# Output projection of a hybrid layer: who makes the low parts of w_out, in which order tile 1's halves run, and when one expert's weights are asked for

## The reference

```python
xn = rmsnorm(x, norm_mix_g) * (1 + sc1) + sh1
y_conv, y_ret = short convolution group, retention group of xn @ w_in      # 512 + 512 columns
out = jnp.concatenate([y_conv, y_ret], axis=-1) @ w_out                   # 1024 x 1024, fp32
x = x + g1 * out
xn = rmsnorm(x, norm_ffn_g) * (1 + sc2) + sh2
x = x + g2 * hier_moe(xn)       # top-1 of 4 groups, then top-2 of its 8 experts; SwiGLU, D_EXPERT 256
```

## Time and profile before

| | |
|---|---|
| time, median of 3 runs | 668.73 us (667.97 to 671.67) |
| the profiled execution's own time | 670.74 us |
| its span in the profile | 669.1 us |
| PE busy | 612.7 us (92%) |
| DVE busy | 318.4 us (48%) |
| ACT busy | 154.1 us (23%) |
| POOL busy | 160.4 us (24%) |
| granted PE clock, mean | 0.968 of full |
| DMA | 183.83 MB, 275 GB/s over the span |

### The profile page before, as it was taken

How to read it: one execution, slowest core, us unless ns; L and a number is a source line. 1 busy time by engine, 2 the same in 40 slices (tenths; PEclk the granted TensorE clock), 3 DMA queues, 4 the chain that set the end, 5 groups by cost and what they waited for, 6 DMA issues and landing times.

```text
span 669.1 us, 9054 instructions
## 1 busy us (share of the span) xinstructions
PE 612.7 (92%) x3712; PEld 437.3 (65%) x3712; DVE 318.4 (48%) x631; ACT 154.1 (23%) x297; POOL 160.4 (24%) x124
## 2 busy tenths in 40 slices
PE   3799999999999989999699899999998788889796
PEld 3579999988888865744588797555554444445342
DVE  1433118706240445718768763455454555334326
ACT  5325432122312233354221111101101000001014
POOL 0042724333242200027330011222221111111110
PEclk9989999999999999999799889999999888899999
DMA  7985240320303269788552798999999999999977
GB/s 278 387 295 219 70 153 1 126 89 37 126 0 126 69 227 394 255 317 323 190 196 89 292 390 331 414 418 418 420 417 417 418 420 417 421 417 418 416 279 299
DMA packets 50381, 183.83 MB, mean 275 GB/s; under 512 B 5861, under 2 KB 6037, under 8 KB 38945
## 3 DMA queue, kind: packets, MB, share of 16 engines
q1 hardware_dynamic: 42156, 161.59, 61.9%
q0 software_dynamic: 7216, 18.99, 7.9%
q10 hardware_dynamic: 964, 2.63, 1.1%
HBM read 172.79 MB, written 16.81 MB: 283 GB/s over the span
## 4 chain that ended last, share of the span: by engine, by line
PE 66%; DMA 20%; DVE 7%; SPq 4%; ACT 2%; issue 1%; DVEq 0%; POOLq 0%; ACTq 0%
PE bank L1138 12%; PE bank L1139 11%; PE bank L1140 11%; PE bank L1488 9%; DMA ring<-in_w_up_e 8%; DMA arena_ab<-in_w_up_e 4%; DMA x<-in_w_up_e 4%; PE bank L1508 4%; PE bank L1097 3%; DMA ring<-expert_out_rows 2%; PE bank L1433 2%; PE bank L1114 2%; DVE out_lo L480 1%; SPq L519 1%; PE bank L1192 1%
## 5 line engine op out<-in xcount | busy, mean ns | idle before, releaser
L1488 PE MATMUL bank<-ring,arena_ab 128*64 128x256 f32 x352 | 83.3, 392 | 10.1 <-DMA ring<-in_w_up_e 9.6
L680 POOL TENSOR_TENSOR w_lo<-ring,w_hi 128x1024 fp32r<-128x1024 f32 x25 | 61.4, 2458 | 112.5 <-ACT w_hi L864 112.5
L1492 PE MATMUL bank<-ring,arena_ab 128*64 128x256 f32 x352 | 83.3, 392 | 0.0
L1488 PEld LDWEIGHTS bank<-ring,arena_ab 128*64 128x64 f32 x352 | 48.9, 141 | 46.8 <-DMA ring<-in_w_up_e 17.5
L1622 DVE TENSOR_TENSOR arena_ab<-arena_ab,bank 64x256 f32<-64x256 f32 x32 | 19.5, 610 | 113.3 <-ACT arena_ab L1045 113.3
L1138 PE MATMUL bank<-arena_ab_r,w_hi 128*128 128x320 f32 x192 | 62.2, 324 | 3.0 <-DVE xn_lo L1622 2.9
L786 POOL DMA_INDIRECT expert_out_rows<-arena_ab,row_out x32 | 32.0, 1001 | 130.9 <-DVE arena_ab L1622 130.9
L1138 PE MATMUL bank<-w_hi,arena_ab_r 128*128 128x512 f32 x160 | 63.3, 396 | 0.0
L1139 PE MATMUL bank<-w_lo,arena_ab_r 128*128 128x512 f32 x160 | 62.9, 393 | 0.0
L1140 PE MATMUL bank<-w_hi,xn_lo 128*128 128x512 f32 x160 | 62.8, 393 | 0.0
L1139 PE MATMUL bank<-xn_lo,w_hi 128*128 128x320 f32 x192 | 59.9, 312 | 0.0
(11 more groups left out here) (289 smaller groups left out, 1123.1 us busy)
## 6 DMA issues: line engine op xcount, KB each, us to landing
ring<-in_w_ada SPq DMA_DIRECT2D x11, 2048.0 KB, 12.3
ring<-in_w_down_e SPq DMA_DIRECT2D x22, 1024.0 KB, 25.8
ring<-in_w_gate_e SPq DMA_DIRECT2D x22, 1024.0 KB, 23.1
ring<-in_w_up_e SPq DMA_DIRECT2D x22, 1024.0 KB, 26.0
ring<-in_w_in SPq DMA_DIRECT2D x6, 2048.0 KB, 8.4
arena_ab<-in_w_down_e SPq DMA_DIRECT2D x15, 512.0 KB, 24.0
x<-in_w_gate_e SPq DMA_DIRECT2D x5, 1024.0 KB, 25.8
arena_ab<-in_w_gate_e SPq DMA_DIRECT2D x5, 1024.0 KB, 24.0
```

The source lines that it names most:

```text
L680: pool.tensor_tensor(as_piece(w_lo[p_ % 2], p_), piece_of(w, p_), as_piece(w_hi[p_ % 2], p_), ALU.subtract).then_inc(w_lo_ready, 1)
L1488: pe.matmul(bank[2 + p_][0:BLK, 0:DE], lhs, w_gate(s)[:, kt, :], start=(kt == 0), stop=(kt == KT - 1))
L1492: last = pe.matmul(bank[2 + p_][BLK:2 * BLK, 0:DE], lhs, w_up(s)[:, kt, :], start=(kt == 0), stop=(kt == KT - 1))
```

## The change

All eight low pieces of w_out are made by DVE: four of half 0 after `residual(0, 0)`, four of half 1 after the first product of tile 1. POOL keeps only the low parts of y, and those of tile 1 are written over tile 0's place, once tile 0's products are over. In tile 1 half 1 comes first, as whole fp32 like tile 0, and half 0 follows as split. In tile 2 both halves run before `router_T(1)`. After the last tile `clock(14)` becomes `clock(5)` and `clock_on(5)` becomes `clock_on(2)`. SP asks for expert 2's gate and up (slot 0) before expert 1's (slot 2) and before tile 4's residual rows are stored.

```diff
-        out_low_done = lambda half: (1, 5)[half]
-        y_low_done = lambda t: (3, 7, 9, 11)[t - 1]
+        y_low_done = lambda t: 2 * t
+        split_half = lambda t, half: t >= 2 or (t == 1 and half == 0)
+        turn_of = lambda t, half: 2 * t + (1 - half if t == 1 else half)
@@ y_part: the low part of tile 1 lies in tile 0's place
+            to = 0 if t == 1 else t
             if group == 0:
-                return yconvT[:, :, P * t:P * t + P], yconv_lo[:, :, P * t:P * t + P]
-            return yretT[:, t, :, :], yret_lo[:, t, :, :]
+                return yconvT[:, :, P * t:P * t + P], yconv_lo[:, :, P * to:P * to + P]
+            return yretT[:, t, :, :], yret_lo[:, to, :, :]
@@ SP
             down_part_of(3, 0)
+            released(sp, e_slot[2], FIRST_EXPERT_ITEM)
+            gate_up_of(2)
             released(sp, e_slot[1], FIRST_EXPERT_ITEM)
             gate_up_of(1)
             residual_rows_out(NT - 1)
-            released(sp, e_slot[2], FIRST_EXPERT_ITEM)
-            gate_up_of(2)
@@ POOL, y_low and what follows it
                     pool.wait_ge(high_act, y_high_done(t, group))
+                    if t == 1:
+                        pool.wait_ge(wout_mm, 2)
...
-            pool.wait_ge(high_act, out_high_done(0, 3))
-            pool.wait_ge(wout_mm, 1)
-            out_low_part(pool, 0, 3).then_inc(low_pool, 1)
             y_low(1)
-            pool.wait_ge(high_act, out_high_done(1, 3))
-            pool.wait_ge(wout_mm, 2)
-            for c in (2, 3):
-                out_low_part(pool, 1, c).then_inc(low_pool, 1)
             y_low(2)
@@ PE, project
-                n = 2 * t + half
+                n = turn_of(t, half)
...
-                if t == 1:
+                if n in (3, 5):
                     pe.wait_ge(high_act, out_high_done(half, 3))
-                    pe.wait_ge(low_dve, (3, 5)[half])
-                    pe.wait_ge(low_pool, out_low_done(half))
+                    pe.wait_ge(low_dve, 4 * half + 4)
...
-                    if t >= 1:
+                    if split_half(t, half):
@@ PE, the tiles
-                project(t, 0)
+                project(t, int(t == 1))
...
-                if t == 1:
-                    project(t, 1)
+                if t in (1, 2):
+                    project(t, t - 1)
...
-                elif t != 1:
+                elif t not in (1, 2):
                     project(t, 1)
@@ PE, after the last tile
-            clock(14)
+            clock(5)
             router_T(NT - 1)
...
-            clock_on(5)
+            clock_on(2)
@@ DVE
-                residual(t, 0)
+                residual(t, int(t == 1))
+                if t == 1:
+                    dve.wait_ge(high_act, out_high_done(1, 3))
+                    for c in range(4):
+                        out_low_part(dve, 1, c).then_inc(low_dve, 1)
...
-                    for c in range(3):
+                    for c in range(4):
                         dve.wait_ge(high_act, out_high_done(0, c))
                         out_low_part(dve, 0, c).then_inc(low_dve, 1)
...
-                residual(t, 1)
+                residual(t, int(t != 1))
-                if t == 0:
-                    dve.wait_ge(high_act, out_high_done(1, 1))
-                    for c in range(2):
-                        out_low_part(dve, 1, c).then_inc(low_dve, 1)
```

## The result

The changed kernel takes 667.6 us (median of 20 runs, 663.8 to 671.17), the kernel before, beside it, 669.46 us (20 runs, 667.97 to 672.36). The ratio is 0.9971, with an interval of 0.9958 to 0.9983: about 1.9 us faster, where I had forecast 659.4 (657.1 to 663.2). That is less than the 0.5% which the prediction took as the least that can be told from no change; with 20 runs a side the interval leaves out 1, so a small gain is there. The profiled execution of the changed kernel took 665.88 us with a span of 664.1, 1.7 us less than its median, and that of before took 1.3 us more than its own. The two traces differ by 4.9 us where the medians differ by 1.9, so the traces are read for places and the medians for sizes. One number stands out at once: the runs of the changed kernel spread over 7.4 us, those of before over 4.4.

The account below looks back on a forecast made before the run. The weight stream was taken to bound the end, so expert 6's request, set by PE's work from output projection to expert 0, moves it: -6.8 - 1.3 - 1.2 = -9.3 us from 668.73 gives 659.4 us, range 657.1 to 663.2.

Parts of the forecast that it names:

- The projection: Tiles 0 to 2: reordered halves and DVE's low parts bring `router_T(0)` 7.23 us sooner, less 0.4 in tile 2: -6.8 us.
- SP's order: After the projection: asking for expert 2's gate and up sooner only fills a pause before 381.09, worth 0.
- The first gather: Slower rival at POOL's first gather, chance 0.05: 2.1 MB more ahead in the DMA engines make `gathered_rows` wait, 675.7 us.
- The request for expert 6 sets the end: At expert 0's gate and up: from 410.37 weights pass at a full queue, so the end moves with that request.
- and the same at the end: From expert 0's gate and up to the end: the summed gain of -9.3 us arrives unchanged.
- clock(14) to clock(5) and clock_on(5) to clock_on(2): After the last tile, fewer fillers let the transposes and `ranks(4)` begin sooner: -1.3 and -1.2 us.
- the low-clock stretch: From 382 to 390 us: 3.4 us at 1.2 GHz stay in place, and the transposes falling in cost 0.7 us more.
- the ratio 1.78: Price of the lower clock, from a filler's 0.20 us against 0.1125, applied to the transposes after the last tile.
- the fillers were holding the clock up: Rival after the last tile, chance 0.19: with fewer fillers transposes, router and some row-picking records run at 1.2 GHz; 660.8 to 663.8 us.
- the first cut: clock(14) to clock(5): transposes begin 2.0 us sooner, 0.7 lost to the low clock, -1.3; the clock rival has +0.1.
- The rival's second half: After the last router: half of the 32 row-picking records run at 1.2 GHz and cost 3.0 us more.

Follow-up runs that it names:

- the kernel with the waiting filled: Against the changed kernel: fillers and SP's order as before, but five of clock(14)'s fillers moved into PE's 1.8 us wait for DVE after its last product; 660.75 us.
- 12 fillers late: Changed kernel with the 12 cut fillers put back elsewhere, six each before experts 30 and 31, where PE waits for weights; 664.07 us.
- 4 fillers late: Changed kernel with four fillers (16 PE instructions) added before experts 30 and 31, two each; 665.62 us.
- the pair that leaves the changed kernel out: Changed kernel with clock(14) and clock_on(5) put back, 664.12 us, beside changed kernel with its 5 and 2 fillers widened to 358 and 320 columns, 667.38 us.
- The kernel with one filler added: Changed kernel with a single filler (4 PE instructions) added before expert 30; 666.79 us.

## Why the prediction was wrong, step by step

**The projection, -6.8.** Right in its steps, and 0.9 us too large. Every step is in the trace after: the two fp32 halves, the low parts' 4.6 us for four, POOL off the path, `router_T(0)` at 324.33, 1.30 us from `router_T(1)`'s transposes to its router. Alone it is worth 5.9 us in the median. In the profiled execution 2.0 us are lost again before the slots are free (5.3 sooner instead of 7.3): from about 343 to 347 PE runs at the lower clock, where I had 1.00 up to tile 4. The four profiles with the fillers or SP's order undone (the kernel with the waiting filled is one of them) show no such stretch and free the slots at 362.4 to 362.5; the other six with the projection's change have it. Neither edit acts before that moment, so why it comes and goes stays open.

**SP's order, 0.** Right (0.9998 on the kernel before; 664.12 against 663.76). The first gather was not late, though the DMA share did fall to between 0.03 and 0.36 from 388 to 391 us.

**The request for expert 6 sets the end.** Right while nothing else comes late: from that request to the end it is 258.6 to 259.0 us in five kernels with no stall at the jump, whose requests lie 10.2 us apart. In the three others without a stall it is 259.8 (before, fillers cut), 260.0 (12 fillers late, 1.53 us of them in the chain) and 261.0 (4 fillers late); with the stall it is 260.6 to 264.2. The sum's words "and the same at the end" did not hold for the changed kernel: its request went out 6.85 us sooner, and its span is only 5.0 us shorter. That is the second failed step, below.

**clock(14) to clock(5) and clock_on(5) to clock_on(2), -2.5.** Wrong, and this is the first failed step. With the program's length kept, the cut is worth 0 (664.07 against 664.12). I had the low-clock stretch stay where it was and only transposes fall into it. It grew. The wait before it was longer too, 1.85 us where before had 1.10. (The 0.1125 us that I called a filler there is one record, half a filler; the ratio 1.78 is not touched by it.) The chain after, beside the earlier trace rows:

```profile
380.70 1.97 PE bank L1355 x8
382.68 0.85 PE bank L1419 x4
383.53 2.05 PE bank L1366 x16
385.58 0.34 PE bank L1386 x8
385.92 4.11 PE bank L1429 x16
390.03 0.85 PE bank L1424 x4
...
391.34 7.71 PE bank L1429 x32
```

The transposes take 1.97 us instead of 0.88, two fillers 0.85 instead of 0.45, and later two more 0.85 again: two low stretches, from about 377 to 385 and 387 to 391, 10 us together where there were 6.8. In the same kernel again it was one of 17 us. That was the rival with a chance of 0.19, "the fillers were holding the clock up", and its first half is near to what happened: it had the transposes and the router run at 1.2 GHz and take back the first cut's 2.0 us. In this profile the router (2.05 us, before 1.83) ran mostly at the full clock, in the same kernel again it did not. From the slots' release to the last 32 row-picking records it is 28.4 us before, 26.9 and 28.6 in the two profiles of the changed kernel, and 26.2 and 27.8 in the two with its fillers back: no gain from the cut that stands out of this spread. (The other kernels with the projection's change and short fillers have 26.1 to 26.8; before with its fillers cut has 28.4 again.) The rival's second half was wrong in detail: the 32 row-picking records took 7.71 us again, though before them the clock was low.

**What was not in the sum at all: PE's program at the jump.** The sum carried the gain at expert 6's request to the end unchanged and had nothing for PE's own path there; this is the second failed step, and the larger one. From 664.07 to 668.3 and from 664.12 to 667.38 it costs 3.3 to 4.2 us. The long branch shows in every one of the five profiles with a program 60 or 64 instructions shorter, and in none of the eight others. With the 3.3 us of the pair that leaves the changed kernel out, the sum is -5.9 + 0 + 3.3 = -2.6 us; measured were -1.9 and, again, -1.4. The end of the changed kernel has changed its bound: with the branch at 3.46 us the sums of PE come after the rows instead of before them, and all of PE's lateness there counts.

That the length of the program ahead of the jump decides how long the jump takes is shown. How the wait arises is argued from it. The larger of the two queues for instructions moved 0.51 MB in 31 packets before and 0.49 MB in 30 after, about 16 KB each:

```profile
q8 instruction: 30, 0.49, 0.3%
```

The kernel with one filler added also has 31 packets and stalls, so the count alone does not tell. The Trainium skill (Runtime: NRT & Kernel Launch, section "Instruction fetch mechanics") says that instructions are fetched in order in blocks of 16 KiB, and that a taken branch whose target lies outside the blocks at hand forces a fetch before the engine goes on. By that rule a program shifted by some 48 to 60 instructions could put the target on the far side of a block's border; the packets' 16 KB and the sharp edge agree with it. Where the borders lie, no trace here shows.

## What to carry to other kernels

A cut of instructions also moves everything behind it in the engine's program: where a jump over an unused block stands close to the end, look at the time of the branch itself in both traces before believing any other explanation. Fillers that are to hold the clock are worth trying in the waiting time ahead of its fall first, rather than counting them down. And when one execution's trace shows more gain than the medians, ask which part differs from run to run.

## What the runs showed of the hardware

- One taken branch on PE took 0.36 to 0.74 us in eight profiles and 3.33 to 5.28 us in five, by the number of instructions ahead of it: with 48 fewer than before it was short, with 60 fewer long.
- A wait of 1.83 us after dense matmuls was followed by a granted clock of 0.66 over the next five microseconds, in which fillers ran nearly throughout; with the same stretch broken into a wait of 0.71 us the clock stayed at 1.00. Yet with the fillers back and SP's new order it also stayed at 1.00 over 375 to 380 us, behind a hole as long as that: the wait makes the fall likely, not certain.
- VectorE makes four 128x1024 low parts in 4.6 us, 1.16 us from start to start, while GpSimd takes 1.2 to 2.3 us for one of 128x512.
